# Other order of loads, products and weight tiles in the head of a two-block transformer kernel

## The reference

```python
c_act = jax.nn.silu(c)
mod = c_act @ w_mod[l] + b_mod[l]                    # 1024 -> 6 x 1024
sh1, sc1, gt1, sh2, sc2, gt2 = [m[:, None, :] for m in jnp.split(mod, N_MOD, axis=-1)]
h = rms_norm(x, norm_mix[l]) * (1.0 + sc1) + sh1
p = h @ w_in[l]                                      # 1024 -> 512 + 768 + 1408
p_a, p_b, p_c = jnp.split(p, [P_A, P_A + P_B], axis=-1)
y_a = chunked_sgu(p_a, ...)                          # u, v = split(gelu(p_a)); v normed, mixed in chunks of 128
y_b = rg_lru_block(p_b, ...)                         # xr (conv of 4 taps, gates, scan) and yg (gelu)
y_c = rwkv7_time_mix(p_c, ...)
```

## Time and profile before

| | us |
|---|---|
| median of 3 runs | 2829.52 |
| lowest, highest | 2829.08, 2830.18 |
| the profiled execution: time | 2828.0 |
| its span | 2826.2 |
| PE busy in the span | 2644.1 (94%) |
| DVE busy | 1151.9 (41%) |
| POOL busy | 928.9 (33%) |
| ACT busy | 560.9 (20%) |

### The profile page before, as it was taken

How to read it: one execution, slowest core, us unless ns; L and a number is a source line. 1 busy time by engine, 2 the same in 40 slices (tenths; PEclk the granted TensorE clock), 3 DMA queues, 4 the chain that set the end, 5 groups by cost and what they waited for, 6 DMA issues and landing times.

```text
span 2826.2 us, 35717 instructions
## 1 busy us (share of the span) xinstructions
PE 2644.1 (94%) x15644; PEld 1584.4 (56%) x15644; DVE 1151.9 (41%) x1288; ACT 560.9 (20%) x617; POOL 928.9 (33%) x390
## 2 busy tenths in 40 slices
PE   4869999999899999999998899999889999999996
PEld 1545558886455555555554666776345555555552
DVE  5466666663533310223126665255443220222233
ACT  3225422211211100111003122321131110011102
POOL 0212110000144444444445766101124444444450
PEclk8989999999899999999998999998889999999998
DMA  5432020000011111111113412300001111111101
GB/s 237 164 119 82 20 101 3 3 3 15 30 40 50 54 53 43 45 53 45 62 65 137 58 54 67 119 1 23 30 30 45 53 59 46 44 47 53 59 31 60
DMA packets 44267, 162.65 MB, mean 58 GB/s; under 512 B 4560, under 2 KB 14288, under 8 KB 41168
## 3 DMA queue, kind: packets, MB, share of 16 engines
q1 hardware_dynamic: 38496, 151.21, 16.4%
q10 hardware_dynamic: 5616, 9.17, 1.1%
HBM read 147.77 MB, written 12.58 MB: 57 GB/s over the span
## 4 chain that ended last, share of the span: by engine, by line
PE 87%; DVE 6%; DMA 2%; POOL 2%; issue 1%; ACT 1%; SPq 0%; ACTq 0%; DVEq 0%; POOLq 0%
PE pt L918 17%; PE pt L924 17%; PE pt L921 16%; PE pt L1232 13%; PE pt L561 7%; PE pt L411 3%; PE pt L700 2%; PE pt L1930 2%; PE pt L1936 2%; PE pt L1933 2%; PE pt L344 1%; DVE work L532 1%; DMA work<-in_xT 1%; PE pt L397 1%; PE pt L332 1%
## 5 line engine op out<-in xcount | busy, mean ns | idle before, releaser
L889 POOL TENSOR_TENSOR weights_rounded<-work,cst 128x1024 fp32r<-128x1024 f32 (+1 forms) x120 | 314.8, 2623 | 956.9 <-issue 692.5
L921 PE MATMUL pt<-work,weights_rounded 128*128 128x512 bf16 x1408 | 348.8, 384 | 0.0
L893 POOL TENSOR_TENSOR slots<-work,weights_rounded 128x1024 bf16<-128x1024 f32 (+1 forms) x120 | 337.6, 2813 | 9.4
L921 PEld LDWEIGHTS pt<-work,weights_rounded 128*128 128x128 bf16 x1408 | 125.6, 99 | 183.7 <-issue 66.1
L561 PE MATMUL pt<-work 64*64 64x64 f32 (+5 forms) x4512 | 215.3, 247 | 13.4 <-DVE work L532 12.4
L561 PEld LDWEIGHTS pt<-work 64*64 64x64 f32 (+3 forms) x4512 | 196.7, 144 | 32.3 <-DVE work L532 17.2
L918 PE MATMUL pt<-rounded,weights_rounded 128*128 128x512 f32 x704 | 206.1, 428 | 8.8 <-DVE work L1850 5.2
L918 PE MATMUL pt<-rhs_rounded,weights_rounded 128*128 128x512 f32 x704 | 206.2, 428 | 7.8 <-DVE work L815 4.2
L918 PE MATMUL pt<-hidden_rounded,weights_rounded 128*128 128x512 f32 x704 | 207.5, 427 | 0.0
L1006 DVE SCALAR_TENSOR_TENSOR slots<-pt,par,slots 128x1023 f32<-128x1023 f32 x44 | 56.4, 1283 | 315.7 <-ACT slots L992 315.7
L924 PE MATMUL pt<-hidden_rounded,slots 128*128 128x512 bf16 x704 | 179.9, 387 | 0.0
(11 more groups left out here) (330 smaller groups left out, 3495.0 us busy)
## 6 DMA issues: line engine op xcount, KB each, us to landing
work<-in_w_up SPq DMA_DIRECT2D x88, 512.0 KB, 3.6
work<-in_w_mod SPq DMA_DIRECT2D x11, 2048.0 KB, 8.6
work<-in_w_down SPq DMA_DIRECT2D x32, 704.0 KB, 4.0
slots<-in_w_in SPq DMA_DIRECT2D x31, 512.0 KB, 3.7
slots<-in_w_v SPq DMA_DIRECT2D x10, 512.0 KB, 4.0
work<-in_xT ACTq DMA_DIRECT2D x4, 1024.0 KB, 23.1
x_scratch<-work SPq DMA_DIRECT2D x8, 512.0 KB, 2.7
slots<-in_w_out SPq DMA_DIRECT2D x8, 512.0 KB, 3.4
```

Of the source, the lines that this page charges most:

```text
L889: did(pool, pool.tensor_tensor(w_hi(n, cols).rearrange("p (k n) -> p k n", n=P), w_raw(n, cols).rearrange("p (k n) -> p k n", n=P), const( ...
L893: did(pool, pool.tensor_tensor(w_lo(n, cols), w_raw(n, cols), w_hi(n, cols).bitcast(F32), ALU.subtract), "ffn_w_split")
L921: pe.matmul(out, top_half(w_hi(n, cols))[:, k * P:k * P + P], rhs_lo(k), start=False, stop=False, skip_group_check=True)
```

## The change

- x comes over both queues: ACT issues x tiles 0 to 3 (x_in0, x_in1), SP tiles 4 to 7 (x_in2, x_in3) ahead of its groups of w_mod. Group 3 of w_mod moves from SP to ACT. The squares go in the order of tiles 0, 1, 4, 5, 2, 3, 6, 7.
- A square root of ones on ACT after the squares loads the table that `rstd_act` needs.
- On DVE all four `mod_head` calls stand ahead of the first `scaled(k)`; `rstd_dve` stands between the second and the third. `scaled` and `rhs_split` then go in turn.
- xr0 comes ahead of the two v tiles: in `JOBS1`, in the PSUM order, on PE and on ACT. On DVE its convolution (`conv(0)`) stands ahead of the statistics of v.
- Twelve tail products stand where eight did, and ten more behind `conv(0)`; `conv(1)` stands ahead of the normalisation of v.
- In SP's queue groups 0 and 1 of the tail stand ahead of `load(3)`, groups 2 and 3 ahead of `load(4)`, and groups 4 to 7 each behind one of `load(4)` to `load(7)`.

The diff, its core:

```diff
--- before.py
+++ after.py
...
-        for nm, eng in [("ss1", "act"), ("cs1", "dve"), ("rb1", "dve"), ("uA0", "act"), ("uA1", "act"), ("vA0", "act"),
-                        ("vA1", "act"), ("xr0", "dve"), ("xr1", "dve"), ("xr2", "dve")]:
+        for nm, eng in [("ss1", "act"), ("cs1", "dve"), ("rb1", "dve"), ("uA0", "act"), ("uA1", "act"), ("xr0", "dve"),
+                        ("vA0", "act"), ("vA1", "act"), ("xr1", "dve"), ("xr2", "dve")]:
             use(nm, eng)
...
-        JOBS1 = [("uA0", 0), ("uA1", 1), ("vA1", None), ("vA1", None)] + [(f"xr{i}", 4 + i) for i in range(3)] + [
+        JOBS1 = [("uA0", 0), ("uA1", 1), ("xr0", 4), ("vA1", None), ("vA1", None), ("xr1", 5), ("xr2", 6)] + [
             (f"yg{i}", 7 + i) for i in range(3)] + [(f"c{j}", 10 + j) for j in (9, 10, 0, 3, 6, 1, 4, 7, 2, 5, 8)]
...
             sp.dma_start(w(CB), a["c_rows"]).then_inc(E("c_in"), 16)
-            for q in (2, 3, 0):
+            for q in (2, 3):
+                sp.dma_start(W[:, X + 2 * q:X + 2 * q + 2, :], a["xT"][:, 2 * q:2 * q + 2, :]).then_inc(E(f"x_in{q}"), 16)
+            for q in (2, 0):
                 sp.dma_start(W[:, 16 + 4 * q:20 + 4 * q, :], a["w_mod"][:, 4 * q:4 * q + 4, :]).then_inc(E(f"mod_in{q}"), 16)
...
                     sp.wait_ge(E("w_split"), n - 1)
-                src = a["w_v"][:, n - 2, :] if at is None else a["w_in"][at]
+                src = a["w_v"][:, n - 3, :] if at is None else a["w_in"][at]
                 sp.dma_start(p1_raw(n), src).then_inc(E(f"w_in{n % 2}"), 16)
...
             load(2)
+            load_mod(0)
+            load_mod(1)
+            load(3)
             sp.wait_ge(E("rhs_split"), 8)
...
             sp.dma_start(w(T + 1)[:, 0:512], a["sgu_ln"]).then_inc(E("sgu_in"), 16)
-            load_mod(0)
-            load_mod(1)
-            mod_at = {4: 2, 5: 3, 7: 4, 8: 5, 10: 6, 11: 7}
-            for n in range(3, NJOBS1):
+            load_mod(2)
+            load_mod(3)
+            for n in range(4, NJOBS1):
                 load(n)
-                if n in mod_at:
-                    load_mod(mod_at[n])
+                if n < 8:
+                    load_mod(n)
             after_core_sp(sp)
...
+            proj("xr0")
             for g in range(2):
...
                 if g == 0:
-                    pe.wait_ge(E("w_split"), 4)
+                    pe.wait_ge(E("w_split"), 5)
...
-            for name in ("xr0", "xr1", "xr2"):
+            for name in ("xr1", "xr2"):
                 proj(name)
...
         def _(act):
-            for q in range(4):
+            for q in range(2):
                 act.dma_start(W[:, X + 2 * q:X + 2 * q + 2, :], a["xT"][:, 2 * q:2 * q + 2, :]).then_inc(E(f"x_in{q}"), 16)
...
             act.dma_start(par[:, :], a["vectors"]).then_inc(E("vec_in"), 16)
-            act.dma_start(W[:, 20:24, :], a["w_mod"][:, 4:8, :]).then_inc(E("mod_in1"), 16)
+            for q in (3, 1):
+                act.dma_start(W[:, 16 + 4 * q:20 + 4 * q, :], a["w_mod"][:, 4 * q:4 * q + 4, :]).then_inc(E(f"mod_in{q}"), 16)
...
             did(act, act.activation(w(CB), w(CB), ACT.Silu), "c_act")
-            for k in range(8):
+            for n, k in enumerate((0, 1, 4, 5, 2, 3, 6, 7)):
                 act.wait_ge(E(f"x_in{k // 2}"), 16)
-                did(act, act.activation(w(H + k), w(X + k), ACT.Square), "squares")
+                did(act, act.activation(w(H + n), w(X + k), ACT.Square), "squares")
+            act.wait_ge(E("par_in"), 16)
+            did(act, act.activation(small(RS), const("ones")[:, 0:1], ACT.Sqrt), "act_step")
             row_kept(act, "ss1")
...
                 if name == "vA1":
-                    split_hi(5)
                     split_hi(6)
+                    split_hi(7)
                 elif name in job1:
...
-            for nm, dst in (("uA0", U), ("uA1", U + 1), ("vA0", V), ("vA1", V + 1)):
+            def gelu(nm, dst):
                 filled(act, nm)
...
                 tile_done(nm)
+
+            gelu("uA0", U)
+            gelu("uA1", U + 1)
             for i in range(3):
...
                 if i == 0:
+                    gelu("vA0", V)
+                    gelu("vA1", V + 1)
+                if i == 1:
                     act.wait_ge(E("v_var"), 1)
...
             mod_head(3)
+            rstd_dve(dve, "cs1", 1.0 / D, EPS)
             dve.wait_ge(E("vec_in"), 16)
...
             V_(dve.scalar_tensor_tensor(small(G1, 8), small(MOD + 8, 8), 1.0, col("norm_mix", 0, 8), ALU.add, ALU.mult))
-            rstd_dve(dve, "cs1", 1.0 / D, EPS)
             mod_head(0)
+            mod_head(1)
             filled(dve, "rb1")
-            for k in range(4):
-                scaled(k)
-            mod_head(1)
-            for k in range(8):
-                if k < 4:
-                    scaled(k + 4)
-                dve.wait_ge(E("rhs_hi"), k + 1)
-                V_(dve.scalar_tensor_tensor(lo(HLO, k), w(X + k), small(MOD + k), hi(H + k).bitcast(F32), ALU.add,
-                                            ALU.subtract), "rhs_split")
+            for k in range(9):
+                if k < 8:
+                    scaled(k)
+                if k > 0:
+                    dve.wait_ge(E("rhs_hi"), k)
+                    V_(dve.scalar_tensor_tensor(lo(HLO, k - 1), w(X + k - 1), small(MOD + k - 1),
+                                                hi(H + k - 1).bitcast(F32), ALU.add, ALU.subtract), "rhs_split")
             V_(dve.tensor_scalar(small(OMM, 11), col("rwkv_mu", 0, 11), -1.0, 1.0, ALU.mult, ALU.add))
...
                                  const("causal").unsqueeze(1).to_broadcast([P, 4, P]), ALU.mult), "spatial_masked")
-            mod_tail(8)
+            mod_tail(12)
+
+            def conv_taps(dst, src, name, weights, release):
+
+                for j, c in enumerate(weights):
+                    V_(dve.scalar_tensor_tensor(dst[:, j + 1:], src[:, :S - j - 1], c, dst[:, j + 1:], ALU.mult, ALU.add),
+                       release if j == len(weights) - 1 else "dve_step")
+
+            def conv(i):
+                dve.wait_ge(E("xr_first"), i + 1)
+                conv_taps(w(XR + i), pt(f"xr{i}"), None,
+                          [col("lru_conv_w", 3 * j + i) for j in (2, 1, 0)], "pt_emptied_dve")
+                mod_tail(2)
+
+            conv(0)
+            mod_tail(10)
             dve.wait_ge(E("pt_emptied_act"), ordinal["vA1"])
...
-            def conv_taps(dst, src, name, weights, release):
-
-                for j, c in enumerate(weights):
-                    V_(dve.scalar_tensor_tensor(dst[:, j + 1:], src[:, :S - j - 1], c, dst[:, j + 1:], ALU.mult, ALU.add),
-                       release if j == len(weights) - 1 else "dve_step")
-
-            def conv(i):
-                dve.wait_ge(E("xr_first"), i + 1)
-                conv_taps(w(XR + i), pt(f"xr{i}"), None,
-                          [col("lru_conv_w", 3 * j + i) for j in (2, 1, 0)], "pt_emptied_dve")
-                mod_tail(2)
-
-            conv(0)
+            conv(1)
             dve.wait_ge(E("v_sqrt"), 1)
...
                 V_(dve.tensor_tensor(vv, vv, w(T + 1)[:, at:at + 256].unsqueeze(1).to_broadcast([P, 8, 256]), op), "v_normed")
-            conv(1)
             conv(2)
...
```

More of the change, by code:

```diff
@@ L1965, in _ @@
                         cols = slice((k % 4) * 256, (k % 4) * 256 + 256)
-                        pe.matmul(out, hi(H + k)[:, tok], p1_hi(2 + k // 4)[:, cols], start=(k == 0), stop=False,
+                        pe.matmul(out, hi(H + k)[:, tok], p1_hi(3 + k // 4)[:, cols], start=(k == 0), stop=False,
                                   skip_group_check=True)
@@ L1969, in _ @@
                         cols = slice((k % 4) * 256, (k % 4) * 256 + 256)
-                        pe.matmul(out, lo(HLO, k)[:, tok], top_half(p1_hi(2 + k // 4))[:, cols], start=False, stop=False,
+                        pe.matmul(out, lo(HLO, k)[:, tok], top_half(p1_hi(3 + k // 4))[:, cols], start=False, stop=False,
                                   skip_group_check=True)
@@ L1973, in _ @@
                         cols = slice((k % 4) * 256, (k % 4) * 256 + 256)
-                        ins = pe.matmul(out, top_half(hi(H + k)[:, tok]), p1_lo(2 + k // 4)[:, cols], start=False,
+                        ins = pe.matmul(out, top_half(hi(H + k)[:, tok]), p1_lo(3 + k // 4)[:, cols], start=False,
                                         stop=(k == 7), skip_group_check=True)
                 ins.then_inc(E("pt_filled"), 1)
-            for name in ("xr0", "xr1", "xr2"):
+            for name in ("xr1", "xr2"):
                 proj(name)
@@ L2218, in _ @@
                                  const("causal").unsqueeze(1).to_broadcast([P, 4, P]), ALU.mult), "spatial_masked")
-            mod_tail(8)
-            dve.wait_ge(E("pt_emptied_act"), ordinal["vA1"])
-            vv = W[:, V:V + 2, :].rearrange("p a (b n) -> p (a b) n", n=256)
-            for st in range(8):
-                V_(dve.bn_stats(small(STAT + 16 + 6 * st, 6), vv[:, st, :]))
```

(15 more changed lines are left out.)

## The result

| | before | changed |
|---|---|---|
| median us (4 runs each) | 2829.85 | 2802.23 |
| lowest, highest | 2829.08, 2833.87 | 2799.04, 2804.28 |
| span of the profiled execution | 2826.2 | 2797.3 |
| its PE busy | 2644.1 | 2630.3 |

The ratio is 0.9907, 95% interval 0.9893 to 0.9922: the change is faster. The medians differ by 27.6 us (the ratio makes it 26), where 29.5 was forecast (2800). The profiled execution took 2799.04, against 2799.0 forecast for one like it. The two values of PE busy cannot be compared: the trace of the changed kernel lacks 169 of the 15644 matmul records.

The account below looks back on a forecast made before the run. No engine was taken as full: PE waits for a queue's order ahead of yg1. yg1 at 55.4 + 118.0 = 173.4 against 202.4 wins 29.0 us; 2828.0 - 29.0 = 2799.0, plus 1.5 gives median 2800, range 2791 to 2812.

Parts of the forecast that it names:

- POOL's cost in the sixteen products: Head, before the first scaled tile: POOL's rests of weight tiles 0 and 1 delay DVE 4.0 us, bounds 0 and 6.5.
- Loads by bytes and rows: Head loads: 2.45 us per MiB, queues taking turns row by row; x complete at 15.7, group 2 at 21.1.
- DVE as the path to uA: Head: DVE's products and splits set PE's first uA matmul, at 55.4 in place of 63.7, 8.3 us won.
- The wait for v: Between xr0 and vA0: PE waits about 11 us for v's second weight tile, as long as before.
- The fed tiles and the 20.59 us: From xr1 to the mixes: tiles are loaded in time, so PE's 20.59 us gap before the last mix goes.
- The slack ahead of the first mix: Before the first mix: v's normalisation ends at u+97, 5 to 6 us before it is wanted.
- DVE late behind the mixes: Between mixes and yg1: two operations and two products per mix, 5.05 us, make DVE late; a 2 to 5 us wait.
- The sum: Up to yg1: start at 173.4 against 202.4, 29.0 us won; 2799.0 for one execution, median 2800.
- (a): Rival in the DVE stretches: DVE and POOL miss each other, 4.0, 2.0 and 2.0 fall away, 2792; chance 0.09.
- (b): Rival: a slower chain behind v's tile moves vA0 and v's normalisation 6 to 12 us, 2806 to 2812; chance 0.12.
- (c): Rival: DVE's tail products all take 3.26 us, delaying v's tile and normalisation; slower than before, 2842; chance 0.05.
- (d): Rival: the 20 us gap only moves elsewhere, leaving just the head's 8 us, 2821; chance 0.03.

Follow-up runs that it names:

- the kernel with short rests: Changed kernel with POOL making only 128 of 1024 columns of the rests of weight tiles 0 and 1, the others zero; 2797.78 us, ratio 0.9901 to before.
- the repeat: The changed kernel itself, unaltered, measured again beside the kernel before; 2801.70 us, ratio 0.9908.

## Why the prediction was right, point by point

| step | forecast | measured |
|---|---|---|
| x complete | 15.7 | 16.5 (ACT's squares without a wait from there) |
| group 2, group 3 of w_mod | 21.1, 30.9 | 21.3, 31.3 |
| POOL's cost in the sixteen products | 4.0 | 4.0 (3.24 and 3.23) |
| first scaled tile | 51.4 | 51.8 |
| uA | 55.4 | 55.8 |
| vA0, and the wait ahead of it | 101.0, 11 | 101.75, 10.06 |
| first mix | 158.0 | 158.1 |
| yg1 | 173.4 | 174.2 |
| gain in front of yg1 | 29.0 | 27.7 |

- **Loads by bytes and rows.** Right, and tested by the two kernels that changed only the order of loads. x was complete at 16.5 and group 2 at 21.3, as one rate for both queues says (15.7 and 21.1); with two full rates it would have been about 12. How the two shared, row by row, decided when DVE could start its fifth product. The trace agrees with the Trainium skill, page "DMA: Bandwidth & Descriptors", section "Issuing engines are not separate DMA queues": the second queue gave x no rate, only its place.
- **DVE as the path to uA.** Right; the waits and both stretched products stood where they were put. In the kernel with short rests the products of 3.24 us became products of 1.4 with POOL's long instructions gone. That agrees with the Trainium skill, page "SBUF — State Buffer", section "Who interferes with whom", by which such a VectorE instruction and a reading GpSimd instruction exclude each other.
- **The wait for v.** Right in size. But I called it "an 11 us wait as long as the old one, but with xr0 done", as if that were neutral. It was not: with xr0 behind v it is 5.2, and with xr0 ahead and v's tile early there is none. I had costed xr0's move against the kernel before and not against the same kernel without it.
- **The fed tiles and the 20.59 us.** Right: the rounding of yg2's tile no longer stood in ACT's way, and the mixes ran as one. The slack ahead of the first mix was smaller than the 5 to 6 us given: DVE's two long operations on v took 6.68 in place of 4.62 us, since the POOL rest of yg2's tile fell there, and v was ready at 154.9, 3.2 us ahead.
- **DVE late behind the mixes.** Right in place, and nearly in size (4.5 forecast, 2.05 + 3.06 = 5.1 measured), with one wait missed: ix0 takes the tensor of the second mix and waits too.
- **A term left out.** Behind those waits PE's granted clock fell: 0.75 of full speed from 174.2 to 181, and yg1's first eight matmuls took 3.68 us in place of 2.20. The sum had counted yg1's tile at full speed, and no term stands for the 1.5 us that this cost. They fall behind the start of yg1, so no shorter wait ahead of vA0 could make them up (vA0 itself came 0.75 us later than forecast). That part was still 1.2 us shorter than before; by the traces' records of the clock PE had spent as long at the lower level there before (167.4 us, against 167.5), only at other places.
- **The sum, and how near it came.** The mechanism was right, but the hit to 0.04 us (2799.04 for 2799.0) is luck. yg1 came 0.8 us later than forecast, and the sum set out from 202.4 where PE's timeline starts yg1 at 201.9: 1.3 us of the 29.0 were not there. The 1.2 us behind yg1 covered that in this execution. In the repeat the part behind yg1 took 2626.9 us and the execution 2803.53. The two ratios, 0.9907 and 0.9908, put the gain at 26 us; their intervals still hold the forecast, and what of the shortfall is more than these 1.3 us is not told from scatter.
- **The rivals.** (a), DVE and POOL missing each other, did not happen: POOL hit two products of the head and one of the first twelve behind it, as priced (2.0, 2.0 and 2.1 us more than 1.22), and c9's rest hit an operation between the mixes (1.4 more, where 2.0 were priced). (b) ate part of the slack and no more. (c) needed products of 2.7 us on average; the 24 ahead of v's statistics had two above 3. (d): no wait of that size turned up elsewhere.

## What to carry to other kernels

Where an engine waits 20 us and nothing is full, follow the releaser back until it ends at a load behind another load that waits for something else: the fault is an order in a queue, and the gain can be counted before it is made. When a change moves a job to fill a wait, cost it against the same kernel without that move, since the move can also be what keeps the wait alive: here xr0 ahead of v lost 5.3 us at yg1 as it was done, and is worth 4.3 once v's tile is loaded early. And when a forecast hits to the hundredth, compare its parts before trusting it. Once the queue is mended, look at what the now early engine still does between two releases: two small products between mixes cost PE 4 us.
